# An MoE stage that loads each expert's weights once: experts ordered by load on the chip, in a one-core fp32 kernel

## The chip, the cores and the metric

The kernel runs on one core of one Trainium2 chip. The metric is the device time of one execution in microseconds (us); where several runs are shown, their median counts. The engines are called as in the profile: PE (TensorE's matmuls), PEld (its weight loads), DVE (VectorE), ACT (ScalarE), POOL (GpSimd) and SP (SyncE, which issues the DMAs here).

## What is computed

The reference runs two blocks one after the other on 256 tokens of width 1024, in fp32. The first has two layers (a mixer, cross attention to 256 memory tokens, a feed-forward part each); the second has two layers with attention, spatial gating, convolution and a SwiGLU. The change touches only the feed-forward part of the first block's second layer, a mixture of eight experts of which each token uses the best two:

```python
def moe_swiglu(h, w_router, b_router, w_gate, w_up, w_down):
    logits = (h @ w_router).astype(F32) + b_router.astype(F32)
    top_logits, top_idx = lax.top_k(logits, TOP_K)            # TOP_K = 2
    top_w = jax.nn.softmax(top_logits, axis=-1)
    gates = jnp.sum(jax.nn.one_hot(top_idx, N_EXPERTS, dtype=F32) * top_w[..., None], axis=-2)
    out = jnp.zeros(h.shape, F32)
    for e in range(N_EXPERTS):                                # 8
        y_e = swiglu(h, w_gate[e], w_up[e], w_down[e]).astype(F32)
        out = out + gates[..., e:e + 1] * y_e
    return out.astype(h.dtype)
```

Each expert has three matrices of 1024 x 3584 (the last one transposed), 44 MB in fp32. 256 tokens with two experts each make 512 assignments, so at most three experts can have over 128 tokens.

## The kernel before

fp32 products are made of three fp32r matmuls (`three`, lines 801 to 805): every operand is split into a high half (ACT, `copy` to fp32r, line 1739) and a low half (DVE, the difference, line 3394 for the MoE's weights), and hi*hi, hi*lo and lo*hi are summed in PSUM.

The MoE stage works on *slots*: a slot is one expert with up to 128 of its tokens, gathered by a matmul with a 0/1 selection matrix (`gather`, `build_selection`) and put back by another (`scatter`). There are `SLOTS` = 11 of them: one for each of the eight experts, in the order of their numbers, and `EXTRA` = 3 for the experts with more than 128 tokens. Which expert an extra slot serves is computed on DVE during the first turn (`extra_slots`) and read by SP into registers (`value_load`, line 730) before slot 8. An extra slot loads its expert's weights a second time.

A slot has `PER_SLOT` = 7 *turns*, each for 512 of the 3584 hidden columns: 77 turns in all. A turn uses six *pieces* of 1 MB (128 x 2048 fp32), two each of the gate, up and down matrices: 462 pieces. SP loads them in order (`stream_moe`, `piece`, line 724) into `RAWS` = 4 raw buffers (three in `ring`, one `more_raw`), as soon as `piece_lo` says that DVE is through with the buffer's last piece. ACT's `high(n)` waits for the landing and for PE to have used piece n-4 (`SPLITS` = 4 split buffers), DVE's `low(n)` follows it, and PE waits for `piece_lo`.

On PE a turn g is: `gate` (two pieces, 24 matmuls of 512 columns), `turn(g-1)` (four transposes of the last turn's product), `up` (24 matmuls), `down(g-1)` (24 matmuls into banks 4 and 5), then a side task of a neighbouring slot: the turned selection of the next slot, its gather in two halves, or a quarter of the scatter of the slot before. All side tasks go through PSUM bank 7. The order on each engine is written out by hand in the loops `for g in range(TURNS)` of `pe_moe`, `act_moe` and `dve_moe`; the engines meet by semaphores.

Ahead of the turns stands the router: PE makes the logits and x in token order (line 1565 and 1570), DVE picks two experts for each token, PE counts places with five small matmuls (lines 1575 to 1579), DVE makes ranks and the first selections. The first four weight pieces need nothing of it: their expert is number 0, and SP issues them as soon as the buffers of the stage before are free.

Of the kernel before, what the change touches and what calls it, by code (L numbers as in the profile page):

```python
# [140 lines left out]

def shape_constants():
# [18 lines left out]
    def level(m):  # L161
# [16 lines left out]
        "number": np.broadcast_to(np.arange(NE), (P, NE)),  # L178
    }
# [14 lines left out]
EXTRA = 3  # L194
SLOTS = NE + EXTRA
WIDE = 512
PER_SLOT = FFE // WIDE
TURNS = SLOTS * PER_SLOT
PIECES = 6 * TURNS
RAWS, SPLITS = 4, 4  # L200


# [13 lines left out]
def side_order():  # L216

    out = [("gather", 0, 0), ("gather", 0, 1), ("turn", 0, 0)]
    for s in range(SLOTS):
        if s + 1 < SLOTS:  # L220
            out += [("turn", s + 1, 0), ("gather", s + 1, 0), ("gather", s + 1, 1)]
        if s:
            out += [("scatter", s - 1, part) for part in range(4)]
    return out


SIDE_AT = {which: n + 1 for n, which in enumerate(side_order())}


# [48 lines left out]
def build(nc, small, const, x_t, mem_t, w, out_t):  # L278
    ctx = ExitStack()
    with ctx:  # L280
# [20 lines left out]
        h = sb("h", [P, KT, S])  # L301
        mix = sb("mix", [P, KT, S])
# [19 lines left out]
        extra_expert = over("extra_expert", 63488, [P, 8], I32)  # L322
# [66 lines left out]
        rank_col = route[:, 0:2 * SLOTS].rearrange("p (b s) -> p b s", b=2)  # L389
        gate_col = route[:, 32:32 + 2 * SLOTS].rearrange("p (b s) -> p b s", b=2)  # L390
        gate_row = route[:, 64:67]

        def side_bank_of(which, s, part):

            return ps[:, 1 + part if which == "gather" and s == 0 else 7, :]


# [228 lines left out]
        arena_free = sem("arena_free")  # L626
# [3 lines left out]
        y_summed = sem("y_summed")  # L630
# [5 lines left out]
        gate_silu = sem("gate_silu")  # L636
        prod_done = sem("prod_done")
# [71 lines left out]
        def stream_moe(sp, at):  # L709
            moe = w["moe"].rearrange("(e c p) n -> e c p n", c=6 * PER_SLOT, p=P)  # L710
            known = None

            def piece(n, g, part):
                e, f = divmod(g, PER_SLOT)
                r = n % RAWS
                if n >= RAWS:

                    sp.wait_ge(piece_lo, n - RAWS + 1)
                if n == RING:
                    sp.wait_ge(arena_free, 1)  # L720
                c = 6 * f + part
                src = moe[e, c, :, :] if e < NE else moe[bass.ds(known[e - NE], 1), c, :, :].rearrange(
                    "e p n -> (e p) n")
                sp.dma_start(raw_piece(n), src).then_inc(piece_arrived[r], 16)

            sp.wait_ge(chunk_used, at.n["chunk"])
            for g in range(TURNS):
                if g == NE * PER_SLOT:
                    sp.wait_ge(slots_known, 1)
                    known = [sp.value_load(extra_expert[0:1, i:i + 1], min_val=0, max_val=NE - 1)  # L730
                             for i in range(EXTRA)]
# [826 lines left out]
        def pe_moe(pe, at):  # L1558

            pe.sem_inc(arena_free, 1)  # L1560
# [21 lines left out]
            def side_bank(*which):  # L1582

                n = SIDE_AT[which]
                if n > 1:
                    pe.wait_ge(side_free, n - 1)

            def turn_selection(s):
                side_bank("turn", s, 0)
                pe.wait_ge(sel_built, max(s + 1, 2))  # L1590
                for b in range(2):
                    nc.tensor.transpose(ps[:, 7, b * P:(b + 1) * P], sel[:, s % 2, b, :], cst("ident"))
                for b in range(2):
                    last = mm(ps[:, 7, S:S + 1], sel[:, s % 2, b, :], gate_col[:, b, s:s + 1],
# [3 lines left out]
            def gather(s, half):  # L1598
                if s:
                    side_bank("gather", s, half)  # L1600
                else:
                    pe.wait_ge(sel_built, 1)
                for k in range(4):
                    for b in range(2):
                        last = mm(side_bank_of("gather", s, half)[:, k * P:(k + 1) * P],  # L1605
                                  x_tok[:, b, (4 * half + k) * P:(4 * half + k + 1) * P], sel[:, s % 2, b, :],
# [3 lines left out]
            def scatter(s, part):  # L1610
                if s < SLOTS - 1:
                    side_bank("scatter", s, part)
                    pe.wait_ge(y_out, s + 1)
                else:
                    pe.wait_ge(y_out, s + 1 + part // 2)
                for t in range(2):
                    cs = slice((2 * part + t) * P, (2 * part + t + 1) * P)
                    o = ps[:, 7 if s < SLOTS - 1 else part, t * S:(t + 1) * S]
                    mm(o, y_hi[:, cs], sel_t[:, s % 3, :], start=True, stop=False)
                    last = mm(o, y_lo[:, cs], sel_t[:, s % 3, :], start=False, stop=True)  # L1620
                last.then_inc(side_done, 1)

            def columns(g, bank, n):
                s = g // PER_SLOT
                xs = slice((s % 2) * P, (s % 2) * P + P)
                for part in range(2):

                    pe.wait_ge(piece_lo, n + part + 1)
                    hi, lo = (t.rearrange("p (k n) -> p k n", n=WIDE) for t in split_piece(n + part))
                    for k in range(4):  # L1630
                        xk = 4 * part + k
                        last = three(ps[:, bank, :], (x_hi[:, xk, xs], x_lo[:, xk, xs]), (hi[:, k, :], lo[:, k, :]),
                                     xk == 0, xk == KT - 1)
# [64 lines left out]
            for g in range(TURNS):  # L1698
# [7 lines left out]
                if g:  # L1706
                    down(g - 1)
# [1917 lines left out]
```

## Time and profile before

| | |
|---|---|
| median of three runs | 2874.41 us (2869.45, 2874.41, 2878.86) |
| the profiled execution: time, span | 2878.86 us, 2878.7 us |
| PE busy | 2756.1 us (96%) |
| PEld busy | 2453.9 us (85%) |
| DVE busy | 2185.2 us (76%) |
| ACT busy | 1703.5 us (59%) |
| POOL busy | 116.2 us (4%) |
| read from HBM | 686.53 MB, 239 GB/s over the span |
| of it for the MoE's weights | 347 + 115 issues of 1024.0 KB |

The first three slices in ten of the span belong to the first layer and the second layer's mixer, the MoE's turns run from about 883 to 2250 us, and the second block fills the rest. Times in the rows below are from the span's start. Busy time of PE is that of matmuls which overlap: one of 512 columns is shown with some 0.39 us, and the next begins before it ends. "Idle before" is the time for which an engine had nothing in work ahead of an instruction, with what ended it.

### The profile page before, as it was taken

How to read it: one execution, taken by the hardware profiler on the slowest of the kernel's cores; microseconds unless marked ns; L12 is line 12 of the kernel's file. 1: busy time of each engine (PE TensorE's matmuls, PEld its weight loads, DVE VectorE, ACT ScalarE, POOL GpSimd, SP SyncE). 2: the span in 40 equal slices, each digit the busy share in tenths (PEclk: the TensorE clock that was granted, in tenths of full speed). 3: DMA queues.
4: the chain of work that ended last, by engine and by line, in shares of the span. 5: the costliest groups of instructions: out<-in, count | busy, mean ns of one | idle time of the engine just before them, and what ended most of it. 6: DMA issues, size and time to landing. Idle time of an engine off the chain costs nothing.

```text
span 2878.7 us, 43981 instructions
## 1 busy us (share of the span) xinstructions
PE 2756.1 (96%) x18492; PEld 2453.9 (85%) x18492; DVE 2185.2 (76%) x2158; ACT 1703.5 (59%) x1785; POOL 116.2 (4%) x112
## 2 busy tenths in 40 slices
PE   7778999998999999999999999999999999989998
PEld 6667999987998888888888888888888799989998
DVE  7885655565737888888888888888888668766777
ACT  5314553456646677776767777777776565445543
POOL 7350000000000000000000000000000000000000
PEclk9889999999999999999999999999999999999999
DMA  5103445542527999999999999999999545534553
GB/s 201 60 2 103 159 153 187 187 150 89 162 89 290 343 352 356 347 348 348 359 339 355 349 350 354 346 353 353 347 357 352 199 138 177 190 117 147 176 182 127
DMA packets 238004, 690.42 MB, mean 240 GB/s; under 512 B 10608, under 2 KB 169456, under 8 KB 178416
## 3 DMA queue, kind: packets, MB, share of 16 engines
q1 hardware_dynamic: 235728, 685.52, 66.3%
q8 instruction: 146, 2.39, 0.3%
q10 hardware_dynamic: 2080, 2.10, 0.2%
q14 instruction: 50, 0.41, 0.0%
HBM read 686.53 MB, written 1.05 MB: 239 GB/s over the span
## 4 chain that ended last, share of the span: by engine, by line
PE 74%; DVE 10%; DMA 6%; ACT 5%; issue 3%; DVEq 1%; POOL 0%; POOLq 0%; ACTq 0%; SPq 0%
PE ps L803 22%; PE ps L805 21%; PE ps L804 21%; DMA ring<-moe 5%; DVE w_lo L3394 2%; DVE w_lo L1767 2%; PE ps L1605 1%; DVE more_lo L3394 1%; ACT arena L1736 1%; PE ps L841 1%; ACT w_hi L1751 1%; PE ps L1657 1%; PE ps L1046 1%; PE ps L950 1%; DVEq L2496 1%
## 5 line engine op out<-in xcount | busy, mean ns | idle before, releaser
L1767 DVE TENSOR_TENSOR w_lo<-ring,w_hi 128x1024 fp32r<-128x1024 f32 x362 | 446.5, 1249 | 264.9 <-ACT w_hi L1751 258.8
L1751 ACT ACTIVATE w_hi<-ring 128x1024 fp32r<-128x1024 f32 x362 | 379.8, 1057 | 384.4 <-PE ps L805 364.2
L1739 ACT ACTIVATE w_hi<-ring 128x2048 fp32r<-128x2048 f32 x232 | 445.3, 1919 | 174.5 <-DMA ring<-moe 160.6
L3394 DVE TENSOR_TENSOR w_lo<-ring,w_hi 128x2048 fp32r<-128x2048 f32 x232 | 523.0, 2285 | 27.9 <-ACT w_hi L1739 27.2
L803 PE MATMUL ps<-x_hi,w_hi 128*128 128x256 f32 x1600 | 459.9, 287 | 16.3 <-DVE w_lo L1767 7.4
L804 PE MATMUL ps<-x_lo,w_hi 128*128 128x256 f32 x1600 | 454.4, 284 | 0.0
L805 PE MATMUL ps<-x_hi,w_lo 128*128 128x256 f32 x1600 | 454.3, 284 | 0.0
L803 PEld LDWEIGHTS ps<-x_hi,w_hi 128*128 128x128 f32 x1600 | 308.5, 193 | 22.8 <-issue 16.9
L804 PEld LDWEIGHTS ps<-x_lo,w_hi 128*128 128x128 f32 x1600 | 308.6, 193 | 0.4
L805 PEld LDWEIGHTS ps<-x_hi,w_lo 128*128 128x128 f32 x1600 | 308.5, 193 | 0.0
L1739 ACT ACTIVATE more_hi<-ring 128x2048 fp32r<-128x2048 f32 x115 | 220.8, 1920 | 122.8 <-DMA ring<-moe 117.1
L803 PE MATMUL ps<-w_hi,x_hi 128*128 128x512 f32 (+1 forms) x712 | 273.9, 385 | 2.9 <-DVE w_lo L3394 1.5
L3394 DVE TENSOR_TENSOR more_lo<-ring,more_hi 128x2048 fp32r<-128x2048 f32 x115 | 262.6, 2284 | 11.3 <-ACT more_hi L1739 11.2
L805 PE MATMUL ps<-w_hi,x_lo 128*128 128x512 f32 (+1 forms) x712 | 268.6, 377 | 0.0
L804 PE MATMUL ps<-w_lo,x_hi 128*128 128x512 f32 (+1 forms) x712 | 268.2, 377 | 0.0
L3394 DVE TENSOR_TENSOR more_lo<-more_raw,more_hi 128x2048 fp32r<-128x2048 f32 x115 | 262.8, 2286 | 6.0 <-ACT more_hi L1739 4.6
L803 PE MATMUL ps<-more_hi,x_hi 128*128 128x512 f32 x616 | 247.5, 402 | 2.2 <-DVE more_lo L3394 2.1
L1739 ACT ACTIVATE more_hi<-more_raw 128x2048 fp32r<-128x2048 f32 x115 | 220.9, 1921 | 43.3 <-DMA more_raw<-moe 38.3
L804 PE MATMUL ps<-more_lo,x_hi 128*128 128x512 f32 x616 | 242.9, 394 | 0.0
L805 PE MATMUL ps<-more_hi,x_lo 128*128 128x512 f32 x616 | 242.9, 394 | 0.0
L803 PEld LDWEIGHTS ps<-w_hi,x_hi 128*128 128x128 f32 x712 | 135.3, 190 | 25.7 <-issue 2.3
L805 PEld LDWEIGHTS ps<-w_hi,x_lo 128*128 128x128 f32 x712 | 135.1, 190 | 24.8
(402 smaller groups left out, 5541.0 us busy)
## 6 DMA issues: line engine op xcount, KB each, us to landing
ring<-moe SPq DMA_DIRECT2D x347, 1024.0 KB, 6.5
more_raw<-moe SPq DMA_DIRECT2D x115, 1024.0 KB, 6.9
ring<-ffn_w_up SPq DMA_DIRECT2D x44, 1024.0 KB, 5.1
ring<-ffn_w_down SPq DMA_DIRECT2D x22, 1024.0 KB, 4.8
ring<-xa_w_kv SPq DMA_DIRECT2D x16, 1024.0 KB, 5.5
ring<-w_in SPq DMA_DIRECT2D x16, 1024.0 KB, 7.0
ring<-da_w_qkv SPq DMA_DIRECT2D x12, 1024.0 KB, 5.2
ring<-ff_w_gate SPq DMA_DIRECT2D x11, 1024.0 KB, 5.3
```

The source lines that it names most:

```text
L803: mm(o, lhs[0], rhs[0], start=start, stop=False)
L804: mm(o, lhs[0], rhs[1], start=False, stop=False)
L805: return mm(o, lhs[1], rhs[0], start=False, stop=stop)
L841: last = mm(ps[:, 4, 0:S], cst("ones"), mix[:, k, :], start=k == 0, stop=k == KT - 1)
L950: last = mm(ps[:, 4 + hd, qb * M:(qb + 1) * M], aq[:, 2 * hd + k, qb * P:(qb + 1) * P], ak[:, 2 * hd + k, :], start=k == 0, stop=k == 1)
L1046: last = mm(ps[32 * t:32 * t + 32, 6 + g // 2, (g % 2) * S:(g % 2) * S + S], cm[:, 4 * g + t, :], (s5b(i, n) if n else s5z(i, 0))[:, q, :] ...
L1605: last = mm(side_bank_of("gather", s, half)[:, k * P:(k + 1) * P], x_tok[:, b, (4 * half + k) * P:(4 * half + k + 1) * P], sel[:, s % 2, b ...
L1657: last = nc.tensor.transpose(ps[:, 6, q * P:(q + 1) * P], prod[:, g % 2, q * P:(q + 1) * P], cst("ident"))
L1739: return nc.scalar.activation(o, i, ACT.Copy, **kw)
L1751: nc.scalar.activation(w_hi[:, half_slot(at, half), :], ring[:, s_, half * 1024:half * 1024 + 1024], ACT.Copy).then_inc(hi_ready, 1)
L1767: nc.vector.tensor_tensor(w_lo[:, i, :], ring[:, s_, half * 1024:half * 1024 + 1024], w_hi[:, i, :], ALU.subtract).then_inc(lo_ready, 1)
L3394: nc.vector.tensor_tensor(lo, raw_piece(n), hi, SUB).then_inc(piece_lo, 1)
```

## The change

After the counts are made, DVE orders the eight experts by their number of tokens (`key`, `above`, `position`), and the stage goes through *places* in the fixed order of ranks 0, 3, 1, 7, 2, 4, 5, 6. A place of rank r needs room for 512/(r+1) tokens at most, so ranks 0, 1 and 2 get two *units* of 128 tokens and the others one: again 11 units, but 8 places. A place has seven turns, 56 in all; each piece is loaded and split once and used by both of its units. Three of the eight places (the first, third and fifth) are such pairs. (`is_packed` is False for all units here: this version has no unit of 64 tokens, and the branches for it emit nothing.) The number of every place's expert is read by SP ahead of the first load. PSUM: gate and up banks alternate by work (unit and turn) as before; the transposes go into the up bank of the same work instead of bank 6, and units alternate between banks 4, 5 and 6, 7 for `down`; side tasks borrow a free bank. The code below is the core of the diff; lines with "..." leave out parts.

```diff
-EXTRA = 3
-SLOTS = NE + EXTRA
-TURNS = SLOTS * PER_SLOT
+TURNS = NE * PER_SLOT
+RANKS = (0, 3, 1, 7, 2, 4, 5, 6)
+def units_of_rank(rank):
+    most = 2 * S // (rank + 1)
+    return [(shift, False) for shift in range(0, min(most, S), P)]
+UNITS = [(place, shift, packed) for place, rank in enumerate(RANKS) for shift, packed in units_of_rank(rank)]
+PLACES = [[u for u, unit in enumerate(UNITS) if unit[0] == place] for place in range(NE)]
+def sides_of(g):
+    place, f = divmod(g, PER_SLOT)
+    if place == 0 and f == 0:
+        return [("turn", u, 0) for u in PLACES[0]]
+    if place and f in (1, 2):
+        return [("scatter", place - 1, 2 * f - 2 + i) for i in range(2)]
+    ahead = PLACES[place + 1] if place + 1 < NE else []
+    if f == 3:
+        return [("turn", u, 0) for u in ahead]
+    if f in (4, 5):
+        return [("gather", u, half) for u in ahead[f - 4:f - 3] for half in range(2)]
+    return []
...
         def stream_moe(sp, at):
...
-                if n == RING:
-                    sp.wait_ge(arena_free, 1)
-                src = moe[e, c, :, :] if e < NE else moe[bass.ds(known[e - NE], 1), c, :, :].rearrange(
-                    "e p n -> (e p) n")
+                src = moe[bass.ds(known[e], 1), c, :, :].rearrange("e p n -> (e p) n")
...
+            sp.wait_ge(slots_known, 1)
+            known = [sp.value_load(expert_of[0:1, units[0]:units[0] + 1], min_val=0, max_val=NE - 1)
+                     for units in PLACES]
...
         def pe_moe(pe, at):
...
+            def columns(g, part, n, bank_of):
+                pe.wait_ge(piece_lo, n + part + 1)
+                hi, lo = (t.rearrange("p (k n) -> p k n", n=WIDE) for t in split_piece(n + part))
+                for w, u in works(g):
+                    xs = x_of(u)
                     for k in range(4):
                         xk = 4 * part + k
+                        last = products(u, ps[:, bank_of(w), :], (xs[0][:, xk, :], xs[1][:, xk, :]),
+                                        (hi[:, k, :], lo[:, k, :]), xk == 0, xk == KT - 1)
+                last.then_inc(piece_used, 1)
...
             def gate(g):
+                pe.wait_ge(side_free, SIDES_BEFORE[g])
+                last_work = works(g)[-1][0]
+                if last_work > 1:
+                    pe.wait_ge(gate_silu, last_work - 1)
+                columns(g, 0, first_piece(g), gate_bank)
+                if g:
+                    turn(g - 1)
+                columns(g, 1, first_piece(g), gate_bank)
             def up(g):
-                if g == 1:
-                    pe.wait_ge(slots_known, 1)
-                if g > 1:
-                    pe.wait_ge(prod_done, g - 1)
-                columns(g, 2 + g % 2, first_piece(g) + 2)
+                last_work = works(g)[-1][0]
+                if last_work > 1:
+                    pe.wait_ge(turned_lo, last_work - 1)
+                for part in range(2):
+                    columns(g, part, first_piece(g) + 2, up_bank)
...
             for g in range(TURNS):
                 gate(g)
-                if g:
-                    turn(g - 1)
                 up(g)
+                sides(g)
                 if g:
                     down(g - 1)
...
         def dve_moe(dve, at):
...
-            low(0)
             dve.wait_ge(route_products, 1)
...
-            low(1)
             dve.wait_ge(route_products, 4)
+            stt(dve, key, ps[:, 3, 2 * NE:3 * NE], 16.0, cst("number"), MUL, SUB)
+            tt(dve, above, repeated(key, [P, NE, NE]), scalars(key, [P, NE, NE]), ALU.is_gt)
+            nc.vector.reduce_sum(position, above, AX)
+            tt(dve, of_unit, repeated(position, wide), scalars(cst("unit_rank"), wide), ALU.is_equal)
+            tt(dve, picked, of_unit, repeated(cst("number"), wide), MUL)
+            nc.vector.reduce_sum(number, picked, AX)
+            nc.vector.tensor_copy(expert_of[:, :], number).then_inc(slots_known, 1)
...
```

How the order moves is seen at three places. First DVE, from the end of the router to the first matmul's needs (`tiny`, `route` and `order_work` hold the router's small numbers, `sel` a selection matrix). Before:

```order
L3464 TENSOR_TENSOR route<-tiny 128x16
L3394 TENSOR_TENSOR w_lo<-ring,w_hi 128x2048
L2499 TENSOR_SCALAR route<-ps 128x16
L2495 TENSOR_TENSOR route<-route 128x16
L2499 TENSOR_SCALAR route<-route 128x2x8
L3410 TENSOR_SCALAR sel<-const_sb,route 128x128
L3411 TENSOR_SCALAR sel<-const_sb,route 128x128
```

And in the changed kernel:

```order
L3602 TENSOR_TENSOR route<-tiny 128x16
L2612 SCALAR_TENSOR_TENSOR route<-ps,const_sb 128x8
L2603 TENSOR_TENSOR order_work<-route 128x64
L3607 TENSOR_REDUCE route<-order_work 128x8
L2603 TENSOR_TENSOR order_work<-route,const_sb 128x88
L2603 TENSOR_TENSOR order_work<-order_work,const_sb 128x88
L3611 TENSOR_REDUCE order_work<-order_work 128x11
L3613 CAST expert_of<-order_work 128x11
L2607 TENSOR_SCALAR route<-ps 128x16
L2603 TENSOR_TENSOR route<-route 128x16
L2603 TENSOR_TENSOR order_work<-order_work,route 128x88
L3618 TENSOR_REDUCE route<-order_work 128x11
```

The low half of the second piece is gone from between, and seven small operations up to the cast stand in its place; seven more come before the first selection.

Second SP, where the MoE's loads begin, after the last load of the memory attention. Before:

```order
L687 DMA ring<-xa_w_o 128x8x256 [waits lo_ready] x4
L724 DMA ring<-moe 128x2048 [waits chunk_used]
L724 DMA ring<-moe 128x2048 x2
L724 DMA more_raw<-moe 128x2048 [waits arena_free]
L724 DMA ring<-moe 128x2048 [waits piece_lo] x3
```

And now:

```order
L771 DMA ring<-xa_w_o 128x8x256 [waits lo_ready] x4
L808 TENSOR_LOAD expert_of [waits slots_known,chunk_used]
L808 ISA x2
L808 TENSOR_LOAD expert_of
L808 ISA x2
```

After eight such pairs of rows comes the first load. It now stands behind `slots_known`, the cast on DVE, and behind eight reads of a number.

Third DVE in two turns of the first place, a pair, from the products of one turn to those of the next but one (`act_lo` is what `turned_low` writes, `prod` what `product` writes). Before, turns 0 and 1 of slot 0:

```order
L3430 TENSOR_TENSOR prod<-silu,ps 128x512
L3394 TENSOR_TENSOR more_lo<-ring,more_hi 128x2048
L3394 TENSOR_TENSOR more_lo<-more_raw,more_hi 128x2048
L3435 TENSOR_TENSOR act_lo<-ps,act_hi 128x512
L3394 TENSOR_TENSOR w_lo<-ring,w_hi 128x2048 x2
L3430 TENSOR_TENSOR prod<-silu,ps 128x512
```

Now:

```order
L3561 TENSOR_TENSOR prod<-silu,ps 128x512 x2
L3504 TENSOR_TENSOR more_lo<-more_raw,more_hi 128x2048
L3504 TENSOR_TENSOR w_lo<-ring,w_hi 128x2048 x2
L3504 TENSOR_TENSOR more_lo<-ring,more_hi 128x2048
L3573 TENSOR_TENSOR act_lo<-ps,act_hi 128x512 x2
L3504 TENSOR_TENSOR more_lo<-more_raw,more_hi 128x2048
L3504 TENSOR_TENSOR w_lo<-ring,w_hi 128x2048
L3561 TENSOR_TENSOR prod<-silu,ps 128x512 x2
```

For six low halves there are now two products and two splits of activations. The splits stand behind one low half (`low(n+4)`), whose high half ACT makes once gate part 0 is used.

## Rows read from the trace of the kernel before

**Rows 1.** Stretches: length, busy us (x) by engine, PEclk, DMA share, GB/s.

```profile
883.00:2250.00 1367.00, 1361.23 (x6330) 1120.94 (x6331) 1166.80 (x717) 968.31 (x662) 0.00 (x0) 1.00 0.93 349
1100.00:1860.00 760.00, 757.33 (x3536) 624.61 (x3535) 650.19 (x393) 539.29 (x370) 0.00 (x0) 1.00 0.94 350
1900.00:2200.00 300.00, 298.79 (x1387) 246.00 (x1386) 256.39 (x152) 213.63 (x146) 0.00 (x0) 1.00 0.94 353
```

**Rows 2.** Waits, 883 to 2250 us: who <- releaser: us, times, longest.

```profile
PEld ps L803 <- issue: 10.2, 15, 1.2
PE ps L803 <- DVE w_lo L3394: 3.1, 5, 0.9
PE ps L803 <- DVE more_lo L3394: 2.4, 5, 1.0
```

**Rows 3.** Waits of SP's DMA queue in the same stretch.

```profile
SPq L724 <- DVE w_lo L3394: 602.2, 228, 7.4
SPq L724 <- DVE more_lo L3394: 589.4, 227, 6.5
```

**Rows 4.** Timeline, PE alone (start us, us): near the first weights, and mid-stage.

```profile
883.28 0.39 PE L804 MATMUL ps<-w_lo,x_hi 128*128 128x512 f32 x1
...
885.12 0.39 PE L803 MATMUL ps<-w_hi,x_hi 128*128 128x512 f32 x1
...
1500.06 0.39 PE L804 MATMUL ps<-w_lo,x_hi 128*128 128x512 f32 x1
...
1502.37 0.40 PE L805 MATMUL ps<-more_hi,act_lo 128*128 128x512 f32 x1
```

**Rows 5.** Stretches of two microseconds there, columns as in rows 1.

```profile
883.30:885.30 2.00, 2.00 (x10) 1.66 (x9) 1.30 (x1) 0.67 (x1) 0.00 (x0) 1.00 0.46 193
1500.00:1502.00 2.00, 2.00 (x10) 1.62 (x10) 1.57 (x2) 0.95 (x1) 0.00 (x0) 1.00 1.00 311
```

**Rows 6.** Groups by form, 883 to 2250 us: count, busy, mean ns, idle.

```profile
L3394 DVE TENSOR_TENSOR w_lo<-ring,w_hi 128x2048 fp32r<-128x2048 f32 x228 | 513.9, 2285 | 25.5 <-ACT w_hi L1739 24.9
L1739 ACT ACTIVATE w_hi<-ring 128x2048 fp32r<-128x2048 f32 x228 | 437.6, 1919 | 169.4 <-DMA ring<-moe 155.5 <-PE ps L805 13.6
...
L3435 DVE TENSOR_TENSOR act_lo<-ps,act_hi 128x512 fp32r<-128x512 f32 x76 | 52.5, 690 | 73.7 <-ACT act_hi L1739 73.7
...
L1657 PE MATMUL ps<-const_sb,prod 128*128 128x128 f32 x304 | 45.5, 271 | 0.0
L1739 ACT ACTIVATE act_hi<-ps 128x512 fp32r<-128x512 f32 x76 | 44.9, 590 | 36.9 <-PE ps L1657 36.7
L1605 PE MATMUL ps<-sel,rstd 128*128 128x128 f32 x320 | 38.9, 275 | 0.0
```

**Rows 7.** Timeline of the router and the first slot (start us, us).

```profile
869.35 0.17 DVE L3398 TENSOR_REDUCE tiny<-tiny 128x2 f32<-128x16 f32 x1
869.60 0.17 DVE L2495 TENSOR_TENSOR tiny<-tiny 128x16 f32<-128x16 f32 x1
...
873.47 0.37 PE L1579 MATMUL ps<-route,const_sb 128*128 128x8 f32 x2
...
882.94 0.50 PE L803 MATMUL ps<-w_hi,x_hi 128*128 128x512 f32 x1 [1.41 <-DVE x_lo L3418]
```

**Rows 8.** Source L730 (value loads), and L724, 856 to 859 us.

```profile
L730 SPq TENSOR_LOAD <-extra_expert x3: 263/289/472, 1867.9 to 1869.3; - x3
...
L724 SPq DMA_DIRECT2D ring<-moe x3: 341/432/433, 856.8 to 857.7; - x3
L724 SPq DMA_DIRECT2D more_raw<-moe x1: 646/646/646, 858.3 to 858.3; - x1
...
DMA to landing us min/median/max: 4.8/7.9/10.7
```

**Rows 9.** Short stretches around the router, columns as in rows 1.

```profile
872.60:876.00 3.40, 1.24 (x10) 1.14 (x10) 3.17 (x7) 2.91 (x3) 0.00 (x0) 1.00 0.23 27
876.00:879.40 3.40, 3.24 (x15) 3.27 (x16) 2.95 (x10) 0.00 (x0) 0.00 (x0) 0.50 0.72 282
```

More of the change, by code:

```diff
@@ L213, in down_piece @@
     return 6 * g + 8 if g < TURNS - 1 else PIECES - 2
[L216 to L227, printed above, removed]
+def sides_of(g):
[10 more added lines that the diff above has]
+    return []
+SIDES = [("gather", u, half) for u in PLACES[0] for half in range(2)]
+SIDES_BEFORE = []
+for _g in range(TURNS):
+    SIDES_BEFORE.append(len(SIDES))
+    SIDES += sides_of(_g)
+SIDE_AT = {which: n + 1 for n, which in enumerate(SIDES)}
 def expert_pieces(gate, up, down):
@@ L1616, in scatter @@
                 for t in range(2):
                     cs = slice((2 * part + t) * P, (2 * part + t + 1) * P)
[L1618 to L1629 removed]
+                    o = ps[:, bank, t * S:(t + 1) * S]
@@ L1661, in down, with sides @@
+            def sides(g):
+                for i, (what, n, part) in enumerate(sides_of(g)):
+                    if is_pair(g):
+                        pe.wait_ge(gate_silu, works(g)[i][0] + 1)
+                    if what == "turn":
+                        turn_selection(n, side_bank(g, i))
+                    if what == "gather":
+                        gather(n, part, side_bank(g, i))
+                    if what == "scatter":
+                        scatter(n, part, side_bank(g, i))
             def down(g):
-                s, f = divmod(g, PER_SLOT)
@@ L3506, in dve_moe @@
[L3506 to L3530 removed]
+            tt(dve, first, first, second, ADD)
@@ new lines, in dve_moe @@
+            for b in range(2):
+                tt(dve, picked, of_unit, repeated(first[:, b, :], wide), MUL)
+                nc.vector.reduce_sum(gate_col[:, b, :], picked, AX)
+                dve.drain()
+            dve.drain().then_inc(slots_known, 1)
+            for u in PLACES[0]:
+                for half in range(2):
+                    take_side(("gather", u, half), first_side_bank(u, half))
+            low(0)
+            low(1)
+            for g in range(TURNS):
+                n = first_piece(g)
+                if g > PER_SLOT and g % PER_SLOT == 1:
+                    y_to_low(g // PER_SLOT - 1)
+                low(n + 2)
+                low(n + 3)
+                if g:
+                    low(n + 4)
+                    turned_low(g - 1)
+                join_gate(g)
+                if g:
+                    low(n + 5)
+                if g + 1 < TURNS:
+                    low(first_piece(g + 1))
+                else:
+                    low(PIECES - 2)
+                product(g)
+                for i, which in enumerate(sides_of(g)):
+                    take_side(which, side_bank(g, i))
+                if g % PER_SLOT == 2 and g // PER_SLOT + 1 < NE:
+                    for u in PLACES[g // PER_SLOT + 1]:
+                        build_selection(u)
+                low(first_piece(g + 1) + 1 if g + 1 < TURNS else PIECES - 1)
```

454 lines of the change are left out of this document (248 added, 206 removed).

## The prediction

> **What bounds the kernel now.** I read the stretches first. From 883 to 2250 us the kernel runs the MoE stage, 1367 us of the 2878.7 us span. There PE is busy for 1361.2 us, DVE for 1166.8, ACT for 968.3, and the DMA engines for a share of 0.93 at 349 GB/s [rows 1]. Two resources look full, PE and DMA, and the change takes load from only one of them, so the question is who waits for whom.
>
> In the table of waits PE's matmuls wait 3.1 and 2.4 us for DVE's low halves, ten times in all, and the weight loads wait 10.2 us in 15 places [rows 2]. SP's queue on the other hand stands for 602.2 and 589.4 us waiting until DVE has freed a raw buffer [rows 3]. So the loads are asked for only as fast as PE uses pieces up. How fast they could come is seen where four are issued at once: the first, from 856.8 us, lands after 4.8 us (861.6), the last, from 858.3, after 10.7 (869.0) [rows 8]. Three loads in 7.4 us is 2.47 us a load, or 425 GB/s; the stage takes 1367/462 = 2.96 us a load. The Trainium skill ("DMA: Bandwidth & Descriptors", section "Where 436 GB/s comes from") says that for transfers between HBM and SBUF the HBM side, some 358 GB/s, binds. By it 484 MB take 1353 us, nearly the whole stage, and the change would pay; this trace shows a faster stretch, so I go by the trace.
>
> A busy PE could still be a slow one, so I read its spacing. Eight matmuls of 512 columns begin between 883.28 and 885.12, 0.230 us each, and ten between 1500.06 and 1502.37, 0.231 us each [rows 4]. In the first place the DMA engines are 0.46 busy, in the second 1.00 [rows 5]. The spacing doesn't depend on the transfers. The clock is 1.00 throughout [rows 1], its upper level of 2.4 GHz. **PE sets the time of the stage**: 77 turns of 72 such matmuls are 5544 x 0.2305 = 1278 us, and transposes, gathers and scatters fill nearly all of the rest.
>
> **What the change does, part by part.**
>
> *Loads and splits.* 336 pieces instead of 462: SP issues 126 fewer loads, ACT 126 fewer high halves (1.92 us each), DVE 126 fewer low halves (2.29 us) [rows 6], 242 us and 289 us of work. All of it lies beside PE; I take 0 us for it. The cover is PE's own work, and it stays: with 11 units of 7 turns and 72 matmuls each there are 5544 again, and 308 transposes, 176 gather and 176 scatter matmuls as before. What ACT and DVE save in the three paired places can't be used by anybody.
>
> *The stalls inside the stage.* The 5.5 us for which matmuls wait [rows 2] can go, at most the 10.2 us of the weight loads. Paired turns use a piece in 24 x 0.2305 = 5.5 us, when it takes 2.47 to land, so they won't wait for loads. Five places of single turns keep the old rhythm. I take -3 us, between -10.2 and 0.
>
> *A possible new wait in paired turns.* `up(g)` now waits until both units' activations of turn g-1 are split. From the end of gate part 0, ACT needs 1.92 (a high half ahead of it in the queue), then DVE 2.29 and twice 0.69: 5.6 us [rows 6], with handovers 5.9. ACT's two copies (0.59 each) fit beside DVE's 2.29. PE meanwhile has eight transposes (45.5/304 = 0.15 each, 1.2 us) and 24 matmuls (5.5 us): 6.7 us. It holds by 0.8 us; I take 0, with 5 us as the upper end (0.25 us in each of 20 paired turns). Queued behind is DVE's next low half, wanted a good 11 us later.
>
> *Addresses from registers.* All loads now use an address read from a register; before, only the last 21 turns did. Those run at 353 GB/s and the same PE share as the earlier ones at 350 [rows 1]. 0 us.
>
> *The start.* This is where the change adds something. Before, four pieces had landed by 869 us, under the router, and the first matmul waited only for the gathered tokens, until 882.94 [rows 7]. Now the loads wait for `slots_known`. The counts are done at 873.47 + 0.37 = 873.84 [rows 7]; DVE then has seven small operations up to the cast, at the 0.25 us from 869.35 to 869.60 [rows 7]: 875.6. SP reads eight values. Three of them began from 1867.9 to 1869.3, 0.7 us apart [rows 8]; the later ones are shorter (median 289 ns against 472), so 0.6 each, 4.8 us (3.7 to 5.6): 880.4. Then 4.8 us for the landing, 1.92 and 2.29 for the halves: 889.4, with handovers 889.6. The other path is longer by a little: seven more small operations and a selection (877.8), then 64 gather matmuls instead of 32 at 38.9/320 = 0.12 us [rows 6], 7.8 us, to 885.6. The clock was at 0.50 (1.2 GHz) from 876.0 to 879.4, after a stretch in which PE was busy for 1.24 of 3.40 us [rows 9]; PE is emptier there now, so I add 0.8. After the last copy (0.6) come the high and low half of piece 0, since ACT has them behind the gathers: 886.4 + 0.2 + 0.6 + 1.92 + 2.29 = 891.4. I take 890.9, between the paths' ends of 889.6 and 892.5: **+8.0 us** (+6.7 to +9.6).
> Of this the gather of the second unit, 32 x 0.12 = 3.9 us, is work that is no longer done later: **-3.9 us**. PE idles some 4 us before the first weights, so the clock may fall again. One stretch of 3.4 us at 1.2 GHz, like that before the old start [rows 9], loses 1.7 us; a low clock for the whole first gate part, 24 matmuls, would lose 5.5: **+1.5 us** (0 to +5.5). The 150 more columns of constants and the loss of `extra_slots` on DVE: 0 us, beside loads and PE.
>
> *Sum.* 0 - 3 + 0 + 8.0 - 3.9 + 1.5 = **+2.6 us**. Against the profiled execution's 2878.86 us that is 2881.5. That execution was the slowest of the three shown; against their median, 2874.41, it is **2877.0 us**. The ends are 6.7 - 3.9 - 10.2 = -7.4 and 9.6 - 3.9 + 5.5 + 5 = +16.2.
>
> **The rivals.**
>
> *The loads bound the stage after all.* Then PE's matmuls are stretched by the traffic and would close up where it falls by half. For it speaks the DMA share of 0.93; against it the same spacing at 0.46 and at 1.00, and SP's 1192 us of waiting. PE's weight loads fill 1120.9 of 1367 us [rows 1], 82%, so a matmul could close up to 0.189 us at most: 42 unit-turns x 72 x 0.041 = 124 us, giving 2750 to 2868 us. The Trainium skill ("TensorE: Matmul & The Clock Gate", section "Back-to-back issue gap") gives 518 cycles for 512 columns, 215.7 ns; by it the estimate would be 3024 x 14.8 ns = 45 us, to 2832. Chance with any other gain over 0.3%: 0.07.
>
> *A wait in each paired turn* (slower). Place: PE's first `up` matmul, held by DVE's second `act_lo`. It decides from 0.8 us of lateness in the chain above. If one further high half (1.92 us) gets in front, PE loses 1.1 us in each of 20 turns, +22 us: 2899 us. For it speaks that DVE waited for ACT's `act_hi` for 73.7 us [rows 6]; against it that in paired turns pieces land early. Chance 0.08.
>
> *The start is worse than thought*: loads that share the queues land together, as the last of four did after 10.7 us [rows 8]. Then the first pair of halves comes 5.9 us later: +8.5, 2883 us, with a colder clock 2886. Chance of more than 0.3% slower this way: 0.05.
>
> That the change doesn't load less can be excluded: the program has 336 issues.
>
> **How the numbers follow.** 0.3% of 2874 is 8.6 us, about what a measurement of this kernel can tell from no change. The forecast, with the milder ends of all terms, has 0.80 and lies within it; faster has 0.07, slower 0.08 + 0.05 = 0.13. The range reaches from 2866 (the lower end, -7.4) to 2891 (the upper, +16.2); the rivals beyond it hold less than 0.2.
>
> **What would show it.** The DMA share of the stage falls to near 0.68 and its rate to 255 GB/s while PE stays at 99%; the spacing is 0.23 us in paired turns; DVE and ACT wait more for PE. Two paired turns' `silu` groups are about 35 us apart, single ones 17.5. The first 512-column matmul begins near 891 us. A spacing below 0.225, or over 20 waits of PE for `act_lo`, would prove me wrong.

## The result, and the profile after

The changed kernel takes **2867.15 us** (median of nine runs, 2865.73 to 2875.66); the kernel before, measured beside it, 2876.79 us (nine runs). The ratio is 0.9973, with an interval of 0.9963 to 0.9982: 7.8 us faster by the ratio (5.2 to 10.6), 9.6 in the medians. The profiled execution of the changed kernel is its slowest, 2875.66 us, so that the two traces are only 3.2 us apart. I forecast 2877.0 us and no change.

The stage looks as forecast. Stretches of the changed kernel (length, busy us and count of PE, PEld, DVE, ACT and POOL, granted clock, DMA share, GB/s): the whole stage, a part of the first pair of units, a part of the last, single places.

```profile
887.50:2260.00 1372.50, 1366.81 (x6342) 1126.01 (x6342) 897.71 (x562) 737.84 (x539) 0.00 (x0) 1.00 0.69 254
900.00:1100.00 200.00, 199.46 (x917) 163.88 (x916) 96.63 (x63) 80.64 (x67) 0.00 (x0) 1.00 0.50 180
1950.00:2200.00 250.00, 250.00 (x1170) 206.22 (x1169) 216.16 (x128) 178.49 (x122) 0.00 (x0) 1.00 0.92 350
```

Beside [rows 1] the DMA share falls from 0.93 to 0.69, DVE from 1166.8 to 897.7 us and ACT from 968.3 to 737.8, while PE is as full as before and the stage as long. Both kernels issue their first weight matmul and the last `silu` of the stage 1366.7 us (882.94 to 2249.65) and 1362.3 us (887.57 to 2249.89) apart.

Waits of the changed kernel from 887 to 2260 us (who, releaser: us, times, longest), beside [rows 2] and [rows 3]:

```profile
ACT w_hi L1821 <- PE ps L884: 213.0, 94, 4.5
ACT w_hi L1821 <- DMA ring<-moe: 47.2, 42, 2.6
PEld ps L882 <- issue: 7.5, 5, 5.1
PE ps L882 <- DVE w_lo L3504: 5.5, 2, 4.9
PE ps L882 <- DVE act_lo L3573: 4.1, 3, 1.4
```

The ten small waits of PE for low halves (5.5 us) are gone but for 0.6 us; 4.9 of the 5.5 shown is the wait ahead of the very first weight matmul. In their place stand three for `act_lo`, 4.1 us. ACT now waits more for PE than for landings (213.0 against 47.2 us).

The start, timeline of the changed kernel (start us, us, engine, line, operation; idle before and releaser in brackets):

```profile
868.54 0.17 DVE L2612 SCALAR_TENSOR_TENSOR route<-ps,const_sb 128x8 f32<-128x8 f32 x1 [1.56 <-PE ps L1657]
870.34 0.17 DVE L3613 CAST expert_of<-order_work 128x11 int32<-128x11 f32 x1
...
873.09 9.58 PE L1674 MATMUL ps<-sel,rstd 128*128 128x128 f32 x64 [4.59 <-DVE sel L3522]
...
875.37 1.43 SPq L804 DMA_DIRECT2D ring<-moe  x3
...
882.70 0.60 ACT L1821 ACTIVATE x_hi<-ps 128x512 fp32r<-128x512 f32 x1 [1.19 <-PE ps L1674]
883.19 3.70 ACT L1821 ACTIVATE w_hi<-ring 128x2048 fp32r<-128x2048 f32 x2
...
885.13 4.49 DVE L3504 TENSOR_TENSOR w_lo<-ring,w_hi 128x2048 fp32r<-128x2048 f32 x2 [1.11 <-ACT w_hi L1821]
887.57 0.47 PE L882 MATMUL ps<-w_hi,x_hi 128*128 128x512 f32 x1 [4.90 <-DVE w_lo L3504]
```

```profile
L808 SPq TENSOR_LOAD <-expert_of x8: 261/266/462, 870.6 to 874.7; - x8
```

The line above stands for the eight reads, with their shortest, median and longest time in ns. Short stretches there, columns as above:

```profile
872.00:876.00 4.00, 2.91 (x14) 2.94 (x15) 3.10 (x16) 0.00 (x0) 0.00 (x0) 0.50 0.02 4
880.00:884.00 4.00, 2.66 (x24) 2.47 (x23) 1.81 (x3) 1.90 (x3) 0.00 (x0) 1.00 1.01 426
888.00:892.00 4.00, 4.00 (x13) 3.13 (x12) 4.00 (x3) 3.78 (x3) 0.00 (x0) 0.58 0.80 297
```

The small chain, the reads and the loads come in the order forecast. The loads land early enough; what decides is that ACT makes high(0) only after the last of the gathered copies. After 4.9 us without a matmul PE runs at 1.2 GHz until about 891 us (granted clock 0.58 over the stretch from 888 to 892).

**Where the traces part** is not the stage. The first matmul of the router (line 1565) begins at 862.20 us before; its like in the changed kernel begins at 856.85. By then the changed kernel is 5.35 us ahead, and nothing of the edited stage has run. From there: router to first weight matmul 20.74 us before and 30.72 now, +10.0; first weight matmul to last `silu` -4.4; the tail up to the first matmul without x after the stage (lines 846 and 925) -4.4; the rest -0.5. Together -4.7, the difference of the spans. The tail is an accident of the one execution shown of before:

```profile
2258.97 0.60 PE L1657 MATMUL ps<-const_sb,prod 128*128 128x128 f32 x4
2263.00 0.80 PE L803 MATMUL ps<-w_hi,act_hi 128*128 128x512 f32 x1 [3.43 <-DVE act_lo L3435]
...
2271.24 0.28 PE L1619 MATMUL ps<-sel_t,y_hi 128*128 128x256 f32 x1
```

Its last `down` begins after a wait of 3.43 us, and runs at first at half clock (stretch of before, columns as above):

```profile
2262.00:2267.00 5.00, 4.00 (x9) 3.14 (x10) 1.54 (x3) 0.00 (x0) 0.00 (x0) 0.50 0.69 213
```

From the transposes to the scatter it took 12.3 us; the changed kernel takes 7.8, and the first experiment, which runs the old program, 7.6.

The 5.35 us come from the first layer's feed-forward part. Timeline of PE there, before and then changed (nine steps from the first row to the last of each):

```profile
430.01 0.28 PE L803 MATMUL ps<-m_hi,w_hi 128*128 128x256 f32 x1
...
431.07 0.28 PE L803 MATMUL ps<-m_hi,w_hi 128*128 128x256 f32 x1
```

```profile
429.97 0.28 PE L882 MATMUL ps<-m_hi,w_hi 128*128 128x256 f32 x1
...
430.99 0.28 PE L882 MATMUL ps<-m_hi,w_hi 128*128 128x256 f32 x1
```

The same instruction on the same data begins every 118 ns before and every 113 ns now, at full clock in both. Over all 1031 of them between 400 and 590 us the mean distance from start to start is 118.9 and 113.5 ns: 5.6 us. What the change does to this part is to move its tiles. `const_sb` grew by 150 columns (600 bytes; tiles begin at rounded addresses), and everything allocated behind it (`h`, `mix`, `rstd`, `tiny`, `arena`, of which `m_hi` and `m_lo` are parts) lies 576 bytes further up in each partition.

### The profile page after: what moved, and what is told of

Read it like the earlier page. It is cut to its first block, busy times and chain, and to the rows that moved or that the text cites. A ratio compares the mean times of both kernels' runs of the same rounds, so it can differ in the third digit from the quotient of the medians.

```text
span 2874.0 us, 43697 instructions
## 1 busy us (share of the span) xinstructions
PE 2748.3 (96%) x18492; PEld 2449.0 (85%) x18492; DVE 1908.6 (66%) x2012; ACT 1466.1 (51%) x1659; POOL 117.1 (4%) x112
## 4 chain that ended last, share of the span: by engine, by line
PE 81%; DVE 8%; ACT 4%; issue 2%; DMA 2%; DVEq 2%; POOL 0%; POOLq 0%; ACTq 0%; SPq 0%
PE ps L882 24%; PE ps L884 23%; PE ps L883 23%; DMA ring<-moe 2%; DVE w_lo L1849 1%; PE ps L1674 1%; ACT arena L1818 1%; DVE w_lo L3504 1%; PE ps L1717 1%; PE ps L920 1%; ACT w_hi L1833 1%; PE ps L1125 1%; PE ps L1029 1%; DVEq L2604 1%; DMA ring<-w_in 1%
## 5 line engine op out<-in xcount | busy, mean ns | idle before, releaser
L3504 DVE TENSOR_TENSOR w_lo<-ring,w_hi 128x2048 fp32r<-128x2048 f32 x168 | 384.4, 2291 | 193.8 <-ACT w_hi L1821 193.5
L1821 ACT ACTIVATE w_hi<-ring 128x2048 fp32r<-128x2048 f32 x168 | 321.7, 1916 | 260.2 <-PE ps L884 213.0
L3504 DVE TENSOR_TENSOR more_lo<-ring,more_hi 128x2048 fp32r<-128x2048 f32 x84 | 192.5, 2291 | 109.4 <-ACT more_hi L1821 108.8
L3504 DVE TENSOR_TENSOR more_lo<-more_raw,more_hi 128x2048 fp32r<-128x2048 f32 x84 | 192.3, 2290 | 95.5 <-ACT more_hi L1821 95.2
L882 PE MATMUL ps<-w_hi,x_hi 128*128 128x512 f32 (+1 forms) x544 | 206.2, 379 | 6.0 <-DVE w_lo L3504 5.5
L882 PE MATMUL ps<-more_hi,x_hi 128*128 128x512 f32 x448 | 178.3, 398 | 0.0
L883 PE MATMUL ps<-more_lo,x_hi 128*128 128x512 f32 x448 | 176.8, 395 | 0.0
L884 PE MATMUL ps<-more_hi,x_lo 128*128 128x512 f32 x448 | 176.8, 395 | 0.0
L882 PE MATMUL ps<-act_hi,w_hi 128*128 128x256 f32 x528 | 150.4, 285 | 4.5 <-DVE w_lo L1849 4.5
L883 PE MATMUL ps<-act_lo,w_hi 128*128 128x256 f32 x528 | 150.2, 284 | 0.0
```

The source lines that it names most:

```text
L882: mm(o, lhs[0], rhs[0], start=start, stop=False)
L883: mm(o, lhs[0], rhs[1], start=False, stop=False)
L884: return mm(o, lhs[1], rhs[0], start=False, stop=stop)
L1821: return nc.scalar.activation(o, i, ACT.Copy, **kw)
L3504: nc.vector.tensor_tensor(lo, raw_piece(n), hi, SUB).then_inc(piece_lo, 1)
```

## The experiments

My theory was now that the address of a matmul's operands sets its pitch (the time from its start to the next one's start), and that the sorting itself is worth nothing. The rival: the gain is the sorting's (less traffic, fewer splits), and the earlier part is chance. In all comparisons the kernel before ran beside (medians 2876.34, 2875.52 and 2876.06 us in the three groups of runs: e1 to e4, e5 to e8, e9 to e11).

**e1: the old kernel with the new allocation.** One entry in `shape_constants` of the kernel before; nothing reads it.

```diff
+        "unused": np.zeros((P, 150)),
```

> The old kernel with 150 unused columns of constants, as many as the change adds. They move h and all tiles behind it (the arena with m_hi, more_hi and others) by 576 bytes; the program is the same otherwise. Theory (placement): the changed kernel's first feed-forward part ran 5.4 us shorter because PE's spacing on m_hi fell from 118.9 to 113.5 ns with the new address, so this kernel gains 5 to 6 us on the old one (ratio 0.998) and shows a spacing near 113.5 there. Rival (chance or clock): the 5.4 us come from the clock or from the execution that was profiled; ratio 1.000, spacing near 119.

2867.09 us (12 runs), ratio 0.9973 (0.9961 to 0.9985): the whole gain of the change, from 150 columns that nobody uses, and more than the 5 to 6 us forecast. The stretch of 20 us shows it in the count of matmuls; before:

```profile
430.00:450.00 20.00, 20.00 (x171) 20.00 (x170) 11.50 (x12) 8.03 (x9) 0.00 (x0) 1.00 0.62 193
```

and with the unused columns:

```profile
430.00:450.00 20.00, 20.00 (x176) 20.00 (x175) 12.18 (x14) 8.43 (x9) 0.00 (x0) 1.00 0.58 175
```

**e2: the changed kernel with the old residue.** 112 unused columns more, so that `arena` lies 1024 bytes from where it was before.

```diff
+        "unused": np.zeros((P, 112)),
```

> The changed kernel with 112 unused columns of constants more, so that the arena lies again at the old address modulo 1024 bytes. Placement: it loses what the changed kernel won outside the MoE stage, 5 to 6 us against the changed kernel, and stands at the old kernel's time plus 0 to 3 us (ratio to it 1.000 to 1.001), spacing on m_hi near 119 ns. Rival: as the changed kernel, ratio to the old one 0.997.

2878.10 us (12 runs), ratio 1.0003 (0.9993 to 1.0014), and the count is back at the old one:

```profile
430.00:450.00 20.00, 20.00 (x170) 20.00 (x169) 11.51 (x12) 7.99 (x9) 0.00 (x0) 1.00 0.61 191
```

So with the allocation as it was, **the sorting costs +0.9 us (-2.0 to +4.0)**, against my +2.6. The changed kernel and e1, which share the shift of 576 bytes, stand together as well (2867.15 and 2867.09 us). e1 and e2 together are the answer: the gain belongs to the addresses, and follows them into the kernel without sorting.

**e3: another tile moved.** 64 bytes ahead of `x_hi` in the kernel before, which moves x, act and arena against `w_hi`.

```diff
+        sb("gap", [P, 16])
```

> The old kernel with a gap of 64 bytes ahead of x_hi, so that x and the activations lie 64 bytes off the weights' tiles modulo 128. Placement, if the distance between the stationary and the moving tile modulo 128 is what counts: the 256-column matmuls that now begin 120 ns apart (some 6400 of them) go to about 114 ns and the kernel gains up to 38 us; in the MoE stage (512 columns) the sign is open, between -20 and +25 us. Rival (only m_hi's own address counts): 5 us gain at most from the arena's move by 64 bytes, none elsewhere.

2867.97 us (10 runs), ratio 0.9974 (0.9964 to 0.9985). The 256-column matmuls come closer (119.9 to 117.8 ns with x), those of 512 with `w_hi` and x move apart, from 228 to 233 ns. Timeline at 1500 us, ten steps in 2.34 us:

```profile
1499.86 0.40 PE L804 MATMUL ps<-w_hi,x_hi 128*128 128x512 f32 x1
...
1502.20 0.40 PE L805 MATMUL ps<-w_lo,x_hi 128*128 128x512 f32 x1
```

An address that is good for one shape is bad for the other: of the MoE's 5544 matmuls the half with `w_hi` and `w_lo` gives back a part, and in the trace the stage, from the first weight matmul to the last `silu`, is 10.1 us longer than before (1376.8 against 1366.7). The forecast of up to 38 us and 114 ns missed.

**e4: the traffic put back.** In the paired places each piece is followed by half of itself once more, into tiles that nobody uses then; each extra load waits for the last one.

```diff
+                if is_pair(g):
+                    if extra:
+                        sp.wait_ge(low_rows_out, 16 * len(extra))
+                    extra.append(n)
+                    sp.dma_start(s5_root[:, :, :, :].rearrange("p a b c -> p (a b c)"), src[:, 0:1024]).then_inc(low_rows_out, 16)
```

> The changed kernel with a further load of half a piece (into a tile that nobody reads) for each of the 126 pieces of the paired places, so half of the saved traffic is back. PE bounds the stage: within 2 us of the changed kernel, PE's spacing in paired turns unchanged at 0.228 to 0.233 us. Rival (the saved traffic is where the gain came from): half of the gain on the old kernel is lost, 4 us.

2891.82 us (4 runs), ratio 1.0061 (1.0041 to 1.0080). It is not a clean experiment: SP stands in the extra waits, pieces come late, and PE waits.

```profile
PE ps L888 <- DVE act_lo L3579: 21.1, 6, 6.6
...
SPq L810 <- DMA s_root<-moe: 529.3, 119, 7.8
```

The pitch of the matmuls in paired turns doesn't change (233.3 ns with `more_*` and x, 227.9 with `w_*`). The waits for `act_lo` are 17.0 us longer than the changed kernel's 4.1, its span 16.2 us longer. So the loss is a wait, and traffic doesn't stretch these matmuls. The forecast of within 2 us missed, and the total says nothing more about the theories.

**e5 and e7: both kernels with chosen addresses.** In each, x, act and arena are put 448 bytes (modulo 1024) from `w_hi`; e5 is the changed kernel, e7 that of before (there the second gap is 32 columns; e5's edit is shown).

```diff
+        sb("gap_x", [P, 112])
         x_at = nc.sbuf_base
...
+        sb("gap_h", [P, 144])
         h = sb("h", [P, KT, S])
```

> The changed kernel with 448 bytes free ahead of x_hi and 576 behind the constants: x, activations and arena all lie 448 bytes (modulo 1024) off the weights' tiles w_hi and w_lo, the distance at which m_hi ran at 113.5 ns. Placement, if this distance is what counts: the 256-column matmuls on x_hi and act_hi fall from 120 to about 114 ns (6400 of them, -38 us), in the MoE stage the matmuls on more_hi with x fall from 233 to 228 ns (2770, -14 us), those on w_hi with x rise from 228 to about 230.5 (2770, +7 us): about 45 us below the changed kernel, 2822 us. Rival (m_hi's 113.5 ns has another reason): within 10 us of the changed kernel.

> The old kernel with the same distances as e5 (448 bytes ahead of x_hi, 128 behind the constants). Placement: some 45 us plus the 7.8 of e1 below the old kernel, about 2825 us, and e5 stands within 3 us of it, since sorting the experts is worth nothing in itself. Rival (the sorted order has a worth of its own): e5 is over 5 us faster than this one.

e5: 2849.88 us (5 runs), ratio 0.9908 (0.9894 to 0.9923). e7: 2844.42 us (6 runs), ratio 0.9897 (0.9880 to 0.9915). The kernel before, with two gaps and nothing else, is 31 us faster than it was and 23 us faster than the changed one. Both forecasts, 2822 and 2825 us, missed by 28 and 19 us: the 256-column matmuls came to 117 or 118 ns in most places, not 114. The intervals of e5 and e7 overlap, and their profiled executions took 2850.58 and 2850.70, but this pair doesn't price the sorting a second time. In the traces e5's first weight matmul begins 8.5 us later than e7's (880.81 against 872.33), its stage up to the last `silu` is 11.2 us shorter (1354.7 against 1366.0), and in the last layer, which no edit touches, the matmuls of e7 begin 4.5 ns closer than those of e5, some 6 us in all (see after the table). Timeline of e7, ten steps in 1.18 us; the kernel before needs 1.20 at the same place (2399.89 to 2401.09):

```profile
2399.89 0.28 PE L806 MATMUL ps<-x_lo,w_hi 128*128 128x256 f32 x1
...
2401.07 0.28 PE L807 MATMUL ps<-x_hi,w_lo 128*128 128x256 f32 x1
```

**e6: half the traffic without sorting.** The kernel before, loading only half the columns of each MoE piece from the fifth on: it leaves out half of the MoE's weights, while every matmul and split still runs.

```diff
+                cols = 2048 if n < RAWS else 1024
+                sp.dma_start(raw_piece(n)[:, 0:cols], src[:, 0:cols]).then_inc(piece_arrived[r], 16)
```

> The old kernel with only the first 1024 of each MoE piece's 2048 columns loaded from the fifth piece on (the rest of the buffer keeps old weights, so half of the MoE's weights are left out); all other instructions stay. It takes away half of the stage's traffic, more than the change does. PE bounds the stage: only the 3 to 8 us go in which PE waited for pieces, spacing unchanged at 0.228 to 0.233 us. Rival (loads bound the stage or stretch the matmuls): 45 us and more below the old kernel, spacing under 0.22.

2862.84 us (4 runs), ratio 0.9955 (0.9939 to 0.9972). Stretch of e6, against [rows 1]:

```profile
1400.00:1600.00 200.00, 200.00 (x941) 165.45 (x940) 170.77 (x106) 141.74 (x98) 0.00 (x0) 1.00 0.53 178
```

The pitch stays (232.3 and 228 ns) at 178 GB/s instead of 350, which ends the rival of stretched matmuls. But waits do end: of [rows 2] none is left, neither the matmuls' 5.5 us nor the weight loads' 10.2 (parts of the same stalls). My 3 to 8 us were too few: in the trace the stage, from the first weight matmul to the last `silu`, is 10.7 us shorter (1356.0 against 1366.7). So 5.5 to 10.2 us of the 12.7 in the medians are placed; the rest I can't place.

**e8, e10, e11: other distances in the kernel before.** Gaps of 256, 192 and 320 bytes ahead of `x_hi`, and of 448, 128 and 128 behind `const_sb`. The edit of e10:

```diff
+        sb("gap_x", [P, 48])
         x_at = nc.sbuf_base
...
+        sb("gap_h", [P, 32])
         h = sb("h", [P, KT, S])
```

> The old kernel at another placement, to see what spacing depends on: x_hi 256 bytes off the weights' tiles modulo 1024, the arena 576 off w_hi. If only the distance modulo 128 counted, x_hi with w_hi would stand at 120 ns (256 is 0 modulo 128) and m_hi at 113.5 (576 and 448 are both 64). If the distance modulo 512 or more counts, other values appear.

> The old kernel with x, activations and arena 192 bytes off w_hi (modulo 1024). From the distances seen so far (moving tile minus stationary tile, modulo 512): 256 columns 0: 120, 64: 117.5, 256: 120, 384: 118.9, 448: 113.5 to 117.5 ns; 512 columns (stationary minus moving) 0: 228, 64: 233.3, 128: 232.3, 192: 229, 256: 228.5, 448: 230.5. If only the distance modulo 512 counts, w_hi with x_hi in the MoE stage stands at 229 and more_hi with x_hi at 228; 256 columns at 192 is new, between 113 and 120.

> As e10, with 320 bytes. 256 columns at 320 is new; more_hi with x_hi again at 228 (distance 0), w_hi with x_hi in the MoE stage between 228 and 232. If all placements off 0 and 256 give about 116 to 118 ns in the 256-column parts, the kernel stands 20 to 30 us under the old one.

e8: 2864.37 us, 0.9958 (0.9942 to 0.9974). e10: 2850.05 us, 0.9912 (0.9887 to 0.9938). e11: 2862.67 us, 0.9952 (0.9937 to 0.9967). Mean distance of one start to the next in ns, from the timelines, of such matmuls (x from 590 to 850 us, act from 400 to 590, those of 512 columns from 900 to 2240; each a mean over 500 or more):

```text
gap ahead of x_hi    x, w_hi 256   act, w_hi 256   w_hi, x_hi 512   more_lo, x_hi 512
0    (before)           119.9         119.7            227.9             232.3
0    (e1)               119.9         119.6            228.4             233.5
64   (e3)               117.8         117.8            233.0             232.3
192  (e10)              116.9         113.3            231.7             227.5
256  (e8)               119.9         120.0            228.9             229.2
320  (e11)              117.5         117.8            233.7             227.8
448  (e7)               116.9         117.8            231.8             227.4
```

0 and 256 are bad for 256 columns, 192 and 448 are good for both shapes together, 64 and 320 trade one for the other. Two forecasts missed: e10's `w_hi` with x stands at 231.7 ns, not 229, and e11 gained 13.4 us, not 20 to 30.

The addresses don't explain all. The two layers of the second block run the same matmuls on x and act with `w_hi` and `w_lo`, from the same tiles. In e7 they begin 117.8 ns apart on the mean in the first of them (2400 to 2530 us, 1104 steps) and 113.3 ns in the second (2700 to 2830, 1147 steps). Stretches of e7:

```profile
2410.00:2430.00 20.00, 20.00 (x172) 20.00 (x171) 16.43 (x26) 9.66 (x13) 0.00 (x0) 1.00 0.58 184
2710.00:2730.00 20.00, 20.00 (x179) 20.00 (x178) 16.64 (x23) 9.55 (x12) 0.00 (x0) 1.00 0.56 173
```

and of e5, which has 117.8 ns in both:

```profile
2710.00:2730.00 20.00, 20.00 (x172) 20.00 (x172) 16.14 (x23) 10.50 (x15) 0.00 (x0) 1.00 0.53 174
```

In e7 `m_hi`, `m_lo`, `w_hi` and `w_lo` also lie just where they lie in e1 (448 + 128 = 576 bytes of shift), and the same matmuls between 400 and 590 us begin 117.7 ns apart, not 113.5:

```profile
430.00:450.00 20.00, 20.00 (x172) 20.00 (x171) 11.77 (x13) 7.95 (x8) 0.00 (x0) 1.00 0.61 198
```

With x at a gap of 0 or 256, on the other hand, all seven traces have 120.0 ns in both stretches of the second block. So the placement decides whether 256-column matmuls can begin closer than 120 ns apart; what chooses between 117.8 and 113.3 ns at one placement isn't known. Every kernel has one trace, so whether it changes from execution to execution isn't known either.

**e9: the changed kernel's two own faults mended.** e5, with ACT and DVE making the first halves between the two units' gathers, and `turned` ahead of the next half after a pair.

```diff
-            for n in range(3):
-                high(n)
+                high(u)
+            high(2)
...
+                if after_pair(g):
+                    turned_high(g - 1)
+                    high(n + 4)
+                elif g:
```

(and the same for `low` and `turned_low` on DVE.)

> The kernel of e5 (sorted order, better placement) with two orders changed on ACT and DVE: the halves of the first piece go between the two units' gathers, and in the first turn after a pair the activations of the last turn are split ahead of the next weight piece. It prices two waits that the change brought: PE's wait for w_lo at the first gate should shrink by 1.6 us, the three waits of 1.5 us for act_lo at the end of a pair should go (4.5 us). Theory: 6 us under e5, 2844 us. Rival (these waits only move to the next piece): within 2 us of e5.

2840.53 us (5 runs), ratio 0.9876 (0.9856 to 0.9895), the lowest median of the study. PE's waits from 870 to 2260 us:

```profile
PE ps L888 <- DVE x_lo L3545: 2.8, 1, 2.8
...
PE ps L888 <- DVE act_lo L3582: 1.4, 1, 1.4
```

The first weight matmul waits 2.8 us for the second unit's tokens instead of 4.9 for a low half, and of the waits for `act_lo` one is left, at the last turn. In the traces the stage from the first weight matmul to the last `silu` is 4.9 us shorter than e5's (1349.9 against 1354.7), where 4.5 were forecast for the three waits. But of the 7.0 us between the two spans 6.0 lie behind the stage, where both kernels have the same instructions and the same tile addresses: in the last layer e9 has 113.3 ns and e5 117.8. The interval of e9 only touches e5's and overlaps e7's, so what the reordering adds isn't measured sharply, and a sorted kernel isn't shown to beat an unsorted one with the same gaps.

## Why the prediction was right and wrong

**The step that failed** is one half-sentence: "The 150 more columns of constants ...: 0 us, beside loads and PE." I costed the columns as data to be loaded, and not as a shift of all that lies behind them. e1 measures them alone: -7.8 us by its ratio (-11.2 to -4.3). Of it 5.6 us are the 1031 matmuls shown; some 600 more with `m_hi`, `m_lo`, `d_hi` and `d_lo` before 400 and after 590 us come some 5 ns closer, 3 us; in the MoE stage `more_*` with x lose 1.1 ns each, about 2 us back. The rest, some 1 us, I haven't placed, and the split isn't sharp: in the one trace of e1 the first weight matmul comes 11.7 us earlier than before, the stage is 7.1 us longer (3.3 of it in more waits for low halves), and the tail 6.4 us shorter (4.7 of it the accident of before). No view of before could show the price; but "the address may matter" could have stood in the range with two signs, for it was there to be read that the same form had 120.0 ns with x and 118.9 with m. That 2867.15 us still lies inside my range of 2866 to 2891 is luck: its lower end was made of the stalls and the start, and neither brought the gain. (By its own sum that end is 2874.41 - 7.4 = 2867.0.)

The rest of the sum stands up:

- *Loads and splits, 0 us*: right. PE's pitch is the same within 1.5 ns for each pair of tiles in the changed kernel at 180 and at 350 GB/s, and DVE's 269 us less work had no taker. The Trainium skill ("DMA: Bandwidth & Descriptors", section "Where 436 GB/s comes from") lets the HBM side bind at some 358 GB/s. The stretch of 426 GB/s from 880 to 884 us disagrees, for a core that has the chip to itself.
- *Stalls, -3 us*: the matmuls' went from 5.5 to 0.6 us, the weight loads' from 10.2 to 2.4 (7.5, less the 5.1 at the start): -4.9 to -7.8, more than I took and inside my ends.
- *Paired wait, 0 us*: the mechanism was right and the place was not. In paired turns PE never waits for `act_lo`; it waits in the single turn after each pair, where DVE does `low(n+4)` ahead of two splits, while PE has only one unit's work to cover them. 4.1 us, near my upper 5. One of the three:

```profile
1129.91 0.50 PE L882 MATMUL ps<-more_hi,more_x_hi 128*128 128x512 f32 x1 [1.35 <-DVE act_lo L3573]
```

- *Start, +8.0*: measured +10.0, over my upper 9.6. The path of the loads was right: seven small operations took 2.0 us (868.54 to 870.51) where I had 1.8, the reads came 0.59 us apart where I had 0.6, and the first load was issued at 875.37, 6.9 us after the counts where I had 6.6. My path of the gather was too short: it took 4.6 us from the counts to its first matmul where I had 4.0, then 9.6 us to the last copy (873.09 to 882.70) where I had 8.6. It ran partly at 1.2 GHz (granted clock 0.50 from 872 to 876), ended later than the loads, and ACT had high(0) behind it, as said.
- *Clock, +1.5*: 0.58 over four microseconds after the first weights is 1.7 us lost (4 x 0.42, an estimate).
- *Gather moved, -3.9*: -4.4 from first weight to last `silu`, in which the stalls, the new wait and the clock are included; -3.9 - 4.9 + 4.1 + 1.7 is -3.0, so 1.4 us aren't placed. (I counted 176 gather matmuls; at 32 for each of 11 units they are 352, in both kernels, so nothing hangs on it.)
- *Sum*: +2.6 forecast, +0.9 (-2.0 to +4.0) measured between e2 and before. My 0.80 on no change would have been right for the sorting; the kernel as a whole came out faster, clear of no change, by the allocation, a way that none of the rivals had.

The signs that I named inside the stage came true (DMA share 0.69, 254 GB/s, pitch 0.23 us, three waits for `act_lo`). Only the first weight matmul, at 887.57 instead of near 891 although its path was longer than forecast, pointed at the part ahead of the stage, which ran 5.35 us early. Of the rivals, bound by loads falls (e4, e6), the wait was there at a fifth of its price, and the start was 2.0 us later than forecast, not 5.9. With less traffic the pitch might have closed up; it never did. The Trainium skill ("TensorE: Matmul & The Clock Gate", section "Back-to-back issue gap") gives 518 cycles for 512 columns, some 216 ns, for isolated matmuls, and about 131 ns for a stream of weight loads and matmuls. The traces agree with neither: 227 ns is the smallest mean over the stage of any pair of tiles in any run here.

## What to carry to other kernels

A change that adds a tile or a column moves every tile allocated after it. Before its time is put down to what it does, run the old kernel with the same padding, and the new one with the padding undone. Look also at stretches that the edit doesn't touch: the same tiles ran at two different pitches there. When PE is full, loading less brings little (e6: 12.7 us for half of the stage's traffic), mostly in the few waits for late pieces; look then at each boundary between a step with much cover and one with little.

## What was not expected of the hardware

The distance from one matmul's start to the next depends on where its operands lie in SBUF. For 256 columns it was from 113.3 to 120.0 ns, for 512 from 227 to 234 ns, at full clock, with the same instructions in the same order. Whole kernels of the same work took between 2844.42 and 2876.34 us by two gaps of some hundred bytes. The distance of the two tiles matters (e3 moves x away from `w_hi` but `more_*` along with x, and in the MoE stage only the pitch with `w_hi` and `w_lo` changes), and multiples of 256 bytes were the worst for 256 columns. The placement doesn't fix it alone: with the same addresses the same matmuls stood at 117.8 ns in one layer and 113.3 ns in the next (e7), and e9 differs from e5 in the same way. What chooses between the two, and whether it is a matter of banks, of the weight load beside the matmul or of writes of ACT and DVE to the same places stays open: no run separated them.
